# Down projection of two feed-forward layers: 20 of 22 tiles as seven block products instead of eight, operands refilled in place

## The reference, cut to what matters

```
def swiglu(x, w_gate, w_up, w_down):
    return (jax.nn.silu(x @ w_gate) * (x @ w_up)) @ w_down
...
x = x + 0.5 * swiglu(rmsnorm(x, p['g_ffn1']), p['w1_gate'], p['w1_up'], p['w1_down'])
...
x = x + 0.5 * swiglu(rmsnorm(x, p['g_ffn2']), p['w2_gate'], p['w2_up'], p['w2_down'])
```

## Time and profile before

| | |
|---|---|
| time, median of 3 runs (lowest, highest) | 2227.0 us (2225.72, 2229.63) |
| span of the profiled execution, its own time | 2228.1 us (no other time is known of that execution) |
| granted TensorE clock, mean | 0.991 of full speed |
| PE busy | 2166.5 us (97%), 15020 matmuls |
| DVE, ACT, POOL busy | 1345.7, 712.0, 399.7 us |
| first layer: last quad ends, last group of down starts, next stage starts | 503.02, 720.22, 768.87 us |
| second layer: last quad ends, last group of down starts, end | 1947.70, 2164.72, 2228.1 us |

### The profile page before, as it was taken

One profiled execution on the slowest core, in us unless ns is written; L12 is line 12 of the kernel. 1 busy time (PEld: TensorE's weight loads), 2 busy tenths in 40 slices (PEclk: granted clock), 3 DMA queues, 4 the chain that ended last, 5 costly groups with the idle time before them and its releaser, 6 DMA issues. The chain is left out here.

```text
span 2228.1 us, 37795 instructions
## 1 busy us (share of the span) xinstructions
PE 2166.5 (97%) x15020; PEld 2016.9 (91%) x15020; DVE 1345.7 (60%) x2013; ACT 712.0 (32%) x1270; POOL 399.7 (18%) x427
## 2 busy tenths in 40 slices
PE   6899999999999999989999999999999999999998
PEld 5899999998989888878898887989999999989897
DVE  7966766664423678899526155368766766644234
ACT  6422322322212325547403034154223223222122
POOL 1000000000000256768535321520000000000003
PEclk9999999999999999999999999999999999999999
DMA  3212212116423221153411062312122122164222
GB/s 139 77 59 96 76 58 96 67 59 236 125 67 93 73 96 39 59 143 103 163 38 58 20 246 77 135 40 78 59 96 76 58 96 76 59 232 125 66 72 81
DMA packets 70864, 206.67 MB, mean 93 GB/s; under 512 B 9703, under 2 KB 31207, under 8 KB 63079
## 3 DMA queue, kind: packets, MB, share of 16 engines
q1 hardware_dynamic: 67808, 201.84, 26.7%
q10 hardware_dynamic: 2951, 3.35, 0.4%
HBM read 161.14 MB, written 41.23 MB: 91 GB/s over the span
## 5 line engine op out<-in xcount | busy, mean ns | idle before, releaser
L807 PE MATMUL ps<-act_hi,op_hi 128*128 128x272 f32 x1280 | 370.2, 289 | 10.2 <-ACT p L1528 9.6
L808 PE MATMUL ps<-act_lo,op_hi 128*128 128x272 f32 x1280 | 371.6, 290 | 0.0
L809 PE MATMUL ps<-act_hi,op_lo 128*128 128x272 f32 x1280 | 370.8, 290 | 0.0
L707 POOL TENSOR_TENSOR w_hi<-w_raw,ones 128x256 fp32r<-128x256 f32 x148 | 134.4, 908 | 1033.3 <-DMA w_raw<-in_w_plain 790.6
L807 PE MATMUL ps<-act_hi,w_hi 128*128 128x288 f32 (+1 forms) x864 | 290.4, 336 | 7.3 <-DVE act_lo L1981 2.0
L807 PE MATMUL ps<-hs_hi,dn_hi 128*128 128x288 f32 (+1 forms) x864 | 284.9, 330 | 1.3 <-DVE x L2161 1.1
L809 PE MATMUL ps<-act_hi,w_lo 128*128 128x288 f32 (+1 forms) x864 | 283.9, 329 | 0.0
L808 PE MATMUL ps<-hs_lo,dn_hi 128*128 128x288 f32 (+1 forms) x864 | 282.4, 327 | 0.0
L809 PE MATMUL ps<-hs_hi,dn_lo 128*128 128x288 f32 (+1 forms) x864 | 282.3, 327 | 0.0
L807 PE MATMUL ps<-t_hi,op_hi 128*128 128x272 f32 x960 | 277.2, 289 | 0.2 <-DVE hid_t L2002 0.2
L808 PE MATMUL ps<-t_lo,op_hi 128*128 128x272 f32 x960 | 277.1, 289 | 0.0
(11 more groups left out here) (332 smaller groups left out, 4215.1 us busy)
## 6 DMA issues: line engine op xcount, KB each, us to landing
raw_gu<-in_w_gu SPq DMA_DIRECT2D x40, 1024.0 KB, 5.1
w_raw<-in_w_plain SPq DMA_DIRECT2D x54, 512.0 KB, 3.6
dn_raw<-in_w_dn SPq DMA_DIRECT2D x44, 512.0 KB, 4.2
hid<-hid_o SPq DMA_DIRECT2D x40, 544.0 KB, 3.7
hr<-hid SPq DMA_DIRECT2D x88, 144.0 KB, 2.1
hr<-hid SPq DMA_DIRECT2D x44, 256.0 KB, 2.7
x<-x_keep SPq DMA_DIRECT2D x16, 544.0 KB, 5.1
ck_T<-in_ck SPq DMA_DIRECT2D x8, 1024.0 KB, 7.2
```

The costliest lines, as they stand in the source:

```text
L707: steps.done(pool.tensor_tensor(hi[:, r, :], raw[:, r, :], one, ALU.mult))
L807: pe.matmul(out, wh, ah, start=(first and n == 0), stop=False, skip_group_check=goes_on)
L808: pe.matmul(out, wh, al, start=False, stop=False, skip_group_check=goes_on)
L809: ins = pe.matmul(out, wl, ah, start=False, stop=end, skip_group_check=goes_on)
```

## The change

Tiles 0 to 19 of the hidden layer are now also multiplied by quads, 12 per layer: groups of 8, 8 and 4 tiles (`DOWN_GROUPS` counts them in pairs), 4 pairs of output tiles each (`DOWN_PAIRS`). In the first two groups a step has 24 matmuls as before, in the third 12 (`kh` = 2). Tiles 20 and 21 are done chunk by chunk as the last four were. The contraction halves are the even and the odd tiles of the pairs.

- **Operand sums.** After a pair of hidden tiles is stored, POOL makes four differences of its halves in place in `hid_o` (`pair_sums`), and SP stores them to a new DRAM tensor `hid_t`. SP waits for that store's data in its list ahead of the next weight load.
- **Refill in place.** The moving operands of the seven steps are loaded into the places of `act_lo`, `t1_lo`, `t2_lo`, `t4_lo` (`load_moving`: operand j when step j of the last quad of the group before is done), ACT copies them to the high places (`refill_hi`), DVE subtracts in place (`refill_lo`). A refill of a full group is 128 x 2176 elements per operand, of the third 128 x 1088.
- **Eviction.** p1 and U2 are scaled by 0.5; DVE adds four results from PSUM directly to x (`add_bank`), POOL adds U2 and U3 (kept in `u2` and `p1`) to x (`add_part`), three additions per quad. The next copy to `p1` waits for all three.
- **Weights.** POOL instead of DVE makes the four weight sums of a down quad.

```diff
-DOWN = ((0, 8), (8, 18), (18, 22))
-DOWN_ORDER = (1, 0, 2)
...
+DOWN_GROUPS = ((0, 4), (4, 4), (8, 2))
+DOWN_QUADS = len(DOWN_GROUPS) * (KT // 2)
+ALL_QUADS = QUADS + DOWN_QUADS
+DOWN_PAIRS = (2, 3, 1, 0)
+LAST_K = range(20, 22)
+LAST_ROWS = (2, 3)
...
+            def load_down(f, dq, n):
+                u = Quad(n)
+                g, q, kh = down_of(n)
+                sp.wait_ge(f["w_lo"], upto(f, "w_lo", STEPS * (n - 1)))
+                sp.dma_start(raw_dq[kh][n % 2][:, :, :, :], dq[g][q, :, :, :, :]).then_inc(f[f"raw_in{n % 2}"], 16)
...
+            def load_moving(f, g):
+                p0, kh = DOWN_GROUPS[g]
+                sp.wait_ge(f["t_out"], upto(f, "t_out", 16 * (p0 + kh)))
+                for j in range(STEPS):
+                    sp.wait_ge(f["quad_mm"], upto(f, "quad_mm", STEPS * (QUADS + g * (KT // 2) - 1) + j + 1))
+                    if j >= 3:
+                        sp.wait_ge(*refilled(f, g, j - 3))
+                    sp.dma_start(operand(j, kh)[2], hidden_part(j, p0, p0 + kh))\
+                      .then_inc(f[f"mv_in{j % 3}"], 16)
...
+            def pair_sums(f, v):
+                h = [hid_o[:, m, i * TH:(i + 1) * TH] for m in range(2) for i in range(2)]
+                for n, (to, a, b) in enumerate(((0, 1, 0), (1, 3, 1), (3, 3, 0), (2, 2, 3))):
+                    if n >= 2:
+                        pool.wait_ge(f["t_made"], v + n)
+                    if n == 1:
+                        pool.wait_ge(f["t_made"], v + 1)
+                    pool.tensor_tensor(h[to], h[a], h[b], ALU.subtract).then_inc(f["t_made"], 1)
...
+            def add_part(f, u, n, m, h, part, evicted):
+                g, q, _ = down_of(u.n)
+                if g == 0:
+                    pool.wait_ge(*x_back_again(f, q))
+                pool.wait_ge(f["quad_ev"], u.count(EVICTS, upto(f, "quad_ev", evicted)))
+                row = half(x[:, 2 * q + m, :], h)
+                pool.tensor_tensor(row, row, part[:, :, :], ALU.add).then_inc(f["x_added"], 1)
+            def down_quads(f):
+                for v in range(QUADS - 1, ALL_QUADS):
+                    u, n = Quad(v), Quad(v + 1)
+                    prepare = n.n < ALL_QUADS
+                    if prepare:
+                        kh = n.pairs()
+                        raw = raw_dq[kh][n.n % 2]
+                        s0, s1 = (t[:, 0:kh, :] for t in sums)
+                        pool.wait_ge(f["w_lo"], n.count(STEPS, upto(f, "w_lo", 0)))
+                        pool.wait_ge(f[f"raw_in{n.n % 2}"], n.turn(16, upto(f, f"raw_in{n.n % 2}", 16)))
+                        pool.tensor_tensor(s0, raw[:, 1, 0:kh, :], raw[:, 1, kh:2 * kh, :], ALU.add)\
+                            .then_inc(f["w_sum"], 1)
+                        pool.wait_ge(f["w_sum"], n.count(4, upto(f, "w_sum", 1)))
+                        pool.tensor_tensor(s1, s0, raw[:, 0, 0:kh, :], ALU.subtract).then_inc(f["w_sum"], 1)
...
+                    if u.down():
+                        add_part(f, u, 0, 0, 1, u2, U2)
+                    if prepare:
+                        pool.wait_ge(f["w_lo"], n.count(STEPS, upto(f, "w_lo", 2)))
+                        pool.tensor_tensor(s1, raw[:, 0, kh:2 * kh, :], s1, ALU.subtract).then_inc(f["w_sum"], 1)
+                    if u.down():
+                        add_part(f, u, 1, 1, 0, p1, U3)
+                    if prepare:
+                        pool.wait_ge(f["w_lo"], n.count(STEPS, upto(f, "w_lo", 4)))
+                        pool.tensor_tensor(s0, raw[:, 0, 0:kh, :], raw[:, 1, 0:kh, :], ALU.subtract)\
+                            .then_inc(f["w_sum"], 1)
+                    if u.down():
+                        add_part(f, u, 2, 1, 1, p1, C22)
...
+                    if u.opens_group():
+                        pe.wait_ge(f["mv_lo"], upto(f, "mv_lo", STEPS * u.group() + j + 1))
...
+                if j == 6 and u.down() and u.n == QUADS:
+                    act.wait_ge(f["hid_f"], upto(f, "hid_f", 2 * NC + 4 * (FI - 1)))
+                act.activation(hi, src, ACT.Copy).then_inc(f["w_hi"], 1)
...
+                if u.down() and u.n > QUADS:
+                    act.wait_ge(f["x_added"], upto(f, "x_added", 3 * (u.n - QUADS)))
+                act.activation(p1[:, :, :], ps[:, 0:2, 0:TQ], ACT.Copy, scale=0.5 if u.down() else 1.0)\
+                   .then_inc(f["p1_kept"], 1)
...
+            def refill_hi(f, g, j):
+                act.wait_ge(*refilled(f, g, j))
+                hi, _, raw = operand(j, DOWN_GROUPS[g][1])
+                act.activation(hi, raw, ACT.Copy).then_inc(f["mv_hi"], 1)
...
+                    if u.ends_before_group() and j >= 2:
+                        refill_hi(f, u.group() + 1, j - 2)
+                    if u.ends_before_group() and j == STEPS - 1:
+                        refill_hi(f, u.group() + 1, 5)
+                    if u.opens_group() and j == 0:
+                        refill_hi(f, u.group(), 6)
...
+                def add_bank(m, h, bank):
+                    row = half(x[:, 2 * q + m, :], h)
+                    return dve.scalar_tensor_tensor(out=row, in0=ps[:, 2 * bank:2 * bank + 2, 0:TQ], scalar=0.5, in1=row,
...
+                quad_lo(f, u, s, 6)
+                if u.opens_group():
+                    refill_lo(f, g, 5)
+                made(1)
+                dve.wait_ge(f["p1_kept"], u.count(1, upto(f, "p1_kept", 1)))
+                dve.wait_ge(f["quad_ev"], u.count(EVICTS, upto(f, "quad_ev", 0)))
+                if before:
+                    dve.wait_ge(f["x_added"], upto(f, "x_added", before - 2))
+                with_p1(u2)
+                low(0)
+                if u.opens_group():
+                    refill_lo(f, g, 6)
+                made(2)
+                if g == 0:
+                    dve.wait_ge(*x_back_again(f, q))
+                add_bank(0, 0, 0)
+                low(1)
+                if final:
+                    last_hidden_lo(f, 0)
+                made(3)
+                low(2)
+                refill(0)
+                made(4)
+                with_p1(p1)
+                if before:
+                    dve.wait_ge(f["x_added"], upto(f, "x_added", before))
+                add_bank(1, 1, 2)
+                low(3)
+                refill(1)
+                if final:
+                    last_hidden_lo(f, 1)
+                if u.n in (ALL_QUADS - 3, ALL_QUADS - 2):
+                    last_weights_lo(f, u.n - ALL_QUADS + 3)
+                made(5)
+                dve.wait_ge(f["x_added"], upto(f, "x_added", before + 2))
+                add_bank(1, 0, 3)
+                low(4)
+                refill(2)
+                made(6)
+                add_bank(0, 1, 2)
+                refill(3)
+                low(5)
+                refill(4)
```

More of the change, by code:

```diff
@@ L567, in load_ffn @@
[L567 to L578 removed]
+                    store_hidden(f, i, i * 4 + upto(f, "hid_f", 2 * NC))
@@ L2122, in quad @@
                 quad_lo(f, u, s, 6)
-                if prepare:
+                if prepare and not n.down():
                     quad_sums(f, n, 1 - s)
```

484 lines of the change are left out of this document (226 added, 258 removed).

## The result

| | before | after |
|---|---|---|
| time, median (lowest, highest) | 2226.82 us (2225.72, 2229.63) | 2238.33 us (2236.04, 2239.27) |
| ratio after to before | | 1.0053, 95% interval 1.0041 to 1.0064 |
| span of the profiled execution | 2228.1 us | 2235.8 us (its own time 2237.65 us) |

What follows compares the result with a forecast made beforehand. PE's matmuls in the feed-forward layers were taken as the bound. 61.5 us removed less 46.1 us of waits and tails gains 15.4 us: span 2228.1 to 2212.7, median 2212 us, range 2195 to 2229.

Steps and rivals of the forecast that it cites:

- wait at quad 20: Border from up to down quads, once per layer: PE waits for p1, 8.0 us per layer (7.4 to 8.7).
- wait at quad 24: Border between the two full groups, once per layer: PE waits for p1, 4.5 us (2.0 to 5.4).
- third group: Four half quads per layer: waits at their border and behind it, DVE and POOL almost full, 7.5 us (1.9 to 9.5).
- x comes back: First down quad: DVE can't add C11 until x is reloaded, 0.7 us per layer (0 to 1.5).
- tail behind layer 1: Behind the first layer DVE's eviction, parameters, takes and act_lo outlast PE's stage: wait of 4.0 us (2 to 6).
- tail at the end: At the kernel's very end DVE falls slightly further behind PE: 0.7 us (0 to 2).
- What is removed: Down work per layer falls from 265.85 to 235.1 us; PE gains 61.5 us in both layers.
- Queued behind this on ACT are only things PE wants later: Up to down border: behind the chain to p1, ACT's list holds nothing PE needs sooner; no size given.
- At no cost: the four differences per pair: POOL's four differences per pair (1.36 us each) and SP's wait lie under gate and up quads; cover 4 us.
- DVE and POOL together: In borders and third group they slow each other, less than full exclusion; values taken near the upper bounds.
- Rival C: DVE and POOL pieces wait each other out, all upper bounds hold together: 2224 us (2221 to 2231), chance 0.17.
- D: POOL bounds third group and borders; at 3 us for each of 24 down quads, 2238 us; chance 0.15.

Runs made afterwards that it cites:

- The kernel of 9: The change plus filler matmuls in PE's two long waits, parameters between down quads, first pair's differences after quad 0 with SP loading next weights first: 2214.6 us, 0.9944.
- 4: The change plus 56 and 28 unread filler matmuls while PE waits for p1 at quads 20 and 24 of both layers: 2230.8 us, 1.0018.
- 5: The change, with ACT repeating the copy to p1 6, 8, 10 and 13 times more in undisturbed quads 21, 22, 25, 26: 2280.4 us, 1.0237.
- 1: The change, with ACT copying p1 before refills 4 and 5 at the three borders, and DVE reading U2 before its refills 4 and 5: 2243.3 us, 1.0076.
- 2: The kernel with p1 copied first, plus SP issuing the first two x reloads ahead of the third down quad's weights: 2241.7 us, 1.0064.
- 3: One-input DVE refills, low parts left out of the result: on the kernel with p1 and x early 2199.3 us, 0.9871; on the change 2220.6 us, 0.9976.
- Experiment 6: The change, with DVE's and ACT's recurrence parameters computed between the second and third down quad of layer 1: 2228.2 us, 1.0003.

## Why the prediction was wrong

The prediction's sum, both layers together, and what the trace of the changed kernel has in its place:

| term | forecast, us | measured, us |
|---|---|---|
| wait at quad 20 | 16.0 | 8.0 + 8.0 |
| wait at quad 24 | 9.0 | 4.4 + 4.7 |
| third group | 15.0 | 5.1 + 6.7 |
| x comes back | 1.4 | 0 |
| half clock behind the two waits (layer 1, layer 2) | none | 2.4 + 2.9, 2.0 + 2.5 |
| first quads | 0 | 3.5 + 2.1 |
| tail behind layer 1 (over 24.3) | 4.0 | 15.7 |
| all between that tail and the second layer | none | -3.1 |
| tail at the end (over 39.1) | 0.7 | 4.0 |
| sum | 46.1 | 68.9 |

The gain of 61.5 us less 68.9 is 7.4 us of loss; the spans differ by 7.7 (0.2 of the rest is the second layer's down part, which took 217.02 us and not 217.20). Three steps failed: the clock behind the waits and the first pair of each layer, both put at nothing (9.8 and 5.6 us), and the tail behind layer 1, put at 4.0 us (15.7). The kernel of 9 that undoes the clock, the parameters and the first pair measured 2214.6 us, near the 2212 of the forecast; that it is so near is in part luck, as the other misses cancel (third group 3.2 and x 1.4 us less than forecast, 3.1 less between the layers, whose cause is open; 3.3 more at the end).

- **What is removed** was right: undisturbed down quads took 21.07 us.
- **Borders**: the two waits came out within 0.2 us, and for the reason given, in ACT's list (4.5 was a choice between 2.0 and 5.4). What failed is that the wait was priced as itself. Experiments 4 and 5 show that PE runs at 1.2 GHz behind such a wait, 2.0 to 2.9 us more each time, 9.8 in all. Two rows of the kernel before could have warned. Right behind the very p1 wait of 6.1 us that the prediction names from the earlier trace rows, in quad 0, a step took 5.58 us at a clock of 0.50 with DMA idle (the first line below, not looked up); and the last 24 us, where PE idles between small products, stand at 0.85:

```profile
84.61:90.19 5.58, 5.57 (x24) 5.58 (x25) 5.58 (x7) 2.11 (x2) 0.00 (x0) 0.50 0.02 3
2204.00:2228.10 24.10, 14.60 (x115) 14.09 (x113) 12.89 (x27) 3.89 (x10) 4.00 (x5) 0.85 0.50 181
```

  The Trainium skill, TensorE: Matmul & The Clock Gate, section "Part 1: The HAM clock gate", says that PE's clock is halved after idling and comes back only under load; by that rule the borders of quads 20 and 24 would have had this term, and the trace agrees with 0.52 and 0.50.
- **Queued behind this on ACT are only things PE wants later**: true, but the sentence overlooked that two other chains reach the same point. Experiments 1, 2 and 3 show them: x, and DVE's backlog. They cost nothing in the changed kernel, and made a repair of ACT's order alone useless.
- **At no cost: the four differences per pair.** Right for 18 of the 20 pairs, wrong for the first of each layer, whose cover was not looked up: quad 0 takes 30.77 us instead of 21.08 already before the change, with DVE busy for 29.6 of them, and there is no slack to hide 3 us in. It cost 5.6 us; the first kernel with the measured terms alone, in 9, has it undone.
- **Tails** failed most, and the step that failed is the duration of the parameters, put at 5.5 us. The 5.5 us of parameters were taken from a stretch in which POOL was idle; it started its splits at 725.95, right behind them. With the stage half as long the two run side by side, and 5.5 became 13.7. Experiment 6 gives 10 us back and leaves 5.1 over 24.3. That this is near the forecast 4.0 proves little, as the 4.0 had the parameters in it: without them PE still stands 5.2 us ahead of the next stage, and what holds it there was not tested. The end's 3.3 us beyond the forecast were not tested; its last 23.8 us stand at a clock of 0.78.
- **DVE and POOL together.** At the borders the values taken held; the third group, taken near its upper bound at 7.5 us per layer, came out at 5.1 and 6.7. The prediction read the earlier trace rows as less than a full exclusion. In the changed kernel single pairs do show the full size, in both directions: the one that starts second lasts about as long as what is left of the first plus its own time.

```profile
521.02 2.42 DVE L2220 TENSOR_TENSOR t_lo<-t_raw,t_hi 128x2176 fp32r<-128x2176 f32 x1
521.19 3.39 POOL L810 TENSOR_TENSOR sums<-raw_dq 128x512 f32<-128x512 f32 x1 [14.91 <-DVE dq_lo L2134]
524.66 1.61 POOL L813 TENSOR_TENSOR sums<-sums,raw_dq 128x512 f32<-128x512 f32 x1
525.05 3.50 DVE L2220 TENSOR_TENSOR act_lo<-act_raw,act_hi 128x2176 fp32r<-128x2176 f32 x1
```

  The rule of the Trainium skill that the prediction names, SBUF — State Buffer, section "SBUF: two separate sides" (such a pair exclude each other for the whole instruction), agrees with these rows. DVE's tiny operations in the tail, at 0.55 to 0.66 us beside pieces of 0.73, wait in the same way, also those, 8 of the 15 longer than 0.5 us, that have only one tensor as input. Rival C, which is that rule, was right on single pairs and overshot in the sum: the third group stayed below the 9.5 us that it needs, presumably because fewer pairs meet than its upper bounds assume.
- **Rivals.** None was this case. D had the size, 2238 us, and another mechanism: POOL as the bound of all 24 down quads. Undisturbed quads at 21.07 us and half quads behind the opening one at 10.8 to 11.4 (12.0 once, with a slow step) rule it out. The chance of 0.14 for slower rested on that rival alone; it held nothing for the places that were not looked up (first quads, clock, what POOL does where a stage gets shorter).
